# Moving the decay term of the RG-LRU recurrence (1 - loss) from ScalarE to VectorE

## What is computed

```
r = sigmoid(u @ w_rg + b_rg)
i = sigmoid(u @ w_ig + b_ig)
log_a = -LRU_C * r * softplus(-lru_lambda)
a = exp(log_a)
b = sqrt(-expm1(2 * log_a)) * (i * u)
h[t] = a[t] * h[t-1] + b[t]
lru_out = h * gelu(lru_y)
```

## Time and profile before

| | |
|---|---|
| median of 3 runs | 1619.98 us (1619.85 to 1621.9) |
| the profiled execution | 1621.06 us |
| its span, first to last instruction | 1619.2 us |
| TensorE busy | 1603.6 us, 99% |
| POOL busy | 1234.4 us, 76% |
| DVE busy | 905.0 us, 56% |
| ACT busy | 572.3 us, 35% |
| TensorE clock granted, mean | 0.997 of full |

### The profile page before, as it was taken

One profiled execution on the slowest core, in us unless ns is written; L12 is line 12 of the kernel. 1 busy time (PEld: TensorE's weight loads), 2 busy tenths in 40 slices (PEclk: granted clock), 3 DMA queues, 4 the chain that ended last, 5 costly groups with the idle time before them and its releaser, 6 DMA issues.

```text
span 1619.2 us, 24286 instructions
## 1 busy us (share of the span) xinstructions
PE 1603.6 (99%) x7390; PEld 1327.0 (82%) x7390; DVE 905.0 (56%) x1158; ACT 572.3 (35%) x1078; POOL 1234.4 (76%) x1330
## 2 busy tenths in 40 slices
PE   9999999999999999999999999999999999999997
PEld 7888888888888888888888878888888888788887
DVE  6565646652165666676622579677865558405502
ACT  4787335532226885255422244100010013102100
POOL 5787866777777788777777777788887778877875
PEclk9999999999999999999999999999999999999999
DMA  5445432233344454522333583344422222733632
GB/s 165 131 120 131 132 91 80 74 101 93 97 144 128 121 133 114 166 77 74 92 97 95 150 286 107 97 118 117 119 75 75 65 65 69 245 93 114 222 107 87
DMA packets 121462, 188.86 MB, mean 117 GB/s; under 512 B 13668, under 2 KB 45796, under 8 KB 121380
## 3 DMA queue, kind: packets, MB, share of 16 engines
q1 hardware_dynamic: 97476, 144.03, 32.1%
q10 hardware_dynamic: 23904, 43.79, 8.2%
HBM read 162.73 MB, written 17.56 MB: 111 GB/s over the span
## 4 chain that ended last, share of the span: by engine, by line
PE 90%; DVE 4%; issue 2%; ACT 2%; ACTq 0%; DMA 0%; POOL 0%; DVEq 0%; SPq 0%; POOLq 0%
PE ps L872 14%; PE ps L871 14%; PE ps L870 14%; PE ps L1128 8%; PE ps L1127 8%; PE ps L1129 8%; PE ps L1225 4%; PE ps L1226 4%; PE ps L1227 4%; PE ps L950 1%; PE ps L946 1%; PE ps L947 1%; PE ps L1038 1%; DVE rows L2152 1%; DVE rows_r L2311 1%
## 5 line engine op out<-in xcount | busy, mean ns | idle before, releaser
L688 POOL TENSOR_TENSOR w_lo<-w_raw,w_hi 128x512 fp32r<-128x512 f32 (+2 forms) x374 | 448.3, 1199 | 31.2
L685 POOL TENSOR_SCALAR w_hi<-w_raw 128x512 fp32r<-128x512 f32 (+2 forms) x374 | 242.5, 648 | 194.4 <-PE ps L872 127.3
L872 PE MATMUL ps<-h_hi,w_lo 128*128 128x512 f32 x672 | 263.8, 393 | 0.0
L871 PE MATMUL ps<-h_lo,w_hi 128*128 128x512 f32 x672 | 263.6, 392 | 0.0
L870 PE MATMUL ps<-h_hi,w_hi 128*128 128x512 f32 x672 | 262.1, 390 | 0.7 <-DVE g_h L1950 0.6
L870 PEld LDWEIGHTS ps<-h_hi,w_hi 128*128 128x128 f32 x672 | 126.2, 188 | 28.9 <-DVE g_h L1950 1.5
L871 PEld LDWEIGHTS ps<-h_lo,w_hi 128*128 128x128 f32 x672 | 126.2, 188 | 27.5
L872 PEld LDWEIGHTS ps<-h_hi,w_lo 128*128 128x128 f32 x672 | 126.3, 188 | 26.1
L1127 PE MATMUL ps<-t,w_hi 128*128 128x512 f32 x352 | 138.2, 392 | 0.6 <-POOL w_lo L763 0.5
L1128 PE MATMUL ps<-t,w_hi 128*128 128x512 f32 x352 | 138.7, 394 | 0.0
L1129 PE MATMUL ps<-t,w_lo 128*128 128x512 f32 x352 | 136.6, 388 | 0.0
(11 more groups left out here) (389 smaller groups left out, 4105.7 us busy)
## 6 DMA issues: line engine op xcount, KB each, us to landing
w_raw<-w_f SPq DMA_DIRECT2D x68, 256.0 KB, 3.2
w_raw<-w_step SPq DMA_DIRECT2D x64, 256.0 KB, 2.8
w_raw<-w_b SPq DMA_DIRECT2D x64, 256.0 KB, 3.1
w_raw<-w_d SPq DMA_DIRECT2D x64, 256.0 KB, 2.7
w_raw<-w_a SPq DMA_DIRECT2D x96, 128.0 KB, 2.1
w_raw<-w_q SPq DMA_DIRECT2D x32, 256.0 KB, 3.1
w_raw<-w_o SPq DMA_DIRECT2D x32, 256.0 KB, 3.1
mix_hl<-uc_hl ACTq DMA_DIRECT2D x24, 256.0 KB, 4.7
```

Source lines behind the costliest of these rows:

```text
L685: nc.gpsimd.tensor_scalar(w_hi[:, s, w], w_raw[:, s, w], 1.0, 0.0, ALU.mult, ALU.add).then_inc(w_hi_made, 1)
L688: nc.gpsimd.tensor_tensor(w_lo[:, s, w], w_raw[:, s, w], rd(w_hi[:, s, w]), ALU.subtract).then_inc(w_lo_made, 1)
L871: mm(out, w_hi[:, s, w], x_lo, start=False, stop=False)
L872: last = mm(out, w_lo[:, s, w], x_hi, start=False, stop=(k == total - 1))
```

## The change

The 20 `decay` activations leave ScalarE. DVE computes the same value, `g_r` x (-1) + 1 into `g_a`, with a tensor_scalar between amp and b, and counts `a_made` itself. It waits for `loss_made` and `amp_made` first, because it reads what loss writes and overwrites what amp reads. Nothing else moves, and no DMA is touched.

```
@@ ScalarE @@
-            def decay(h, j):
-
-                act.wait_ge(amp_made, j + KR * h + 1)
-                act.wait_ge(loss_made, j + KR * h + 1)
-                fn(g_a[:], g_r[:], ACT.Identity, bias=one_ap, scale=-1.0).then_inc(a_made, 1)
-
@@ ScalarE, recurrent @@
                     gate_root(h, j - 2)
                     mix(h, j)
-                    decay(h, j - 2)
                     gelu(h, j, n + 6, j % 4)
@@ ScalarE, kvq @@
                     gate_fns(h, 8 + p, n + 4 * p + 2)
                     gate_root(h, 8 + p)
-                    decay(h, 8 + p)
@@ DVE, recurrence @@
                 stt(g_r[:], g_a[:], 1.0, g_r[:], ALU.add, ALU.mult).then_inc(loss_made, 1)
                 stt(g_s[:], g_a[:], 1.0, g_s[:], ALU.add, ALU.mult).then_inc(amp_made, 1)
+                dve.wait_ge(loss_made, J + 1)
                 dve.wait_ge(amp_made, J + 1)
+                ts(g_a[:], g_r[:], -1.0, 1.0, ALU.mult, ALU.add).then_inc(a_made, 1)
                 dve.wait_ge(iu_made, J + 1)
                 stt(uc_of(q), g_s[:], 0.5, uc_of(q), ALU.mult, ALU.mult).then_inc(b_made, 1)
```

More of the change, by code:

```diff
@@ L1424, in gelu @@
                 fn(gy[:, q, :], ps[:, bank, :], ACT.Gelu_apprx_tanh).then_inc(gelu_made, 1)
[L1426 to L1430, removed]
             def lru_out_hi(h, j):
```

## The result

The changed kernel takes 1625.77 us, the median of 8 runs (1623.65 to 1627.36), against 1620.91 us for the kernel before on the same chip (8 runs, 1619.85 to 1621.9). The ratio is 1.003, with a 95% interval of 1.0019 to 1.0041: slower by 4.9 us. The forecast was 1624.2, in a range of 1620.9 to 1627.7, against a kernel before of 1619.98. The profiled execution of the changed kernel took 1624.75 us, with a span of 1622.9, 3.7 more than the 1619.2 of before.

The account below looks back on a forecast made before the run. TensorE was taken to bound the kernel, losing time only where it waits for tile 9's scan. 1.31 + 0.79 = 2.10 us a half, 4.2 us in all, gave a median of 1624.2 us, range 1620.9 to 1627.7.

Parts of the forecast that it names:

- What bounds the kernel: TensorE, 99% busy, waits at the second query tile for DVE's scan of tile 9, ending 0.06 us before the matmul.
- Rival 4: No effect: something else already holds TensorE at the second query tile, so the scan may come later; chance 0.05.
- The removal, and the step loop: Taking 20 decay off ScalarE, and 16 added DVE instructions in tiles 0 to 7: both costed at nothing.
- Rival 2: Faster: free ScalarE closes TensorE's weight-load gaps before the gates, at most 1.2 us back, 1618.8 us; chance 0.05.
- Tile 8: b 0.64 us late, the multiply after scan 8 loses its turn to POOL, 1.31 us late into ScalarE's chain.
- Rival 1: Not slower: DVE and POOL miss each other, +1.4 us, 1621.4; chance 0.18 including what lies up to the forecast.
- Tile 9: Loss, amp and the new instruction queue behind POOL: r + 0.34 us extra, 0.79 us with r 0.45.
- remainder r: Rest of a POOL turn that tile 9's queueing instructions meet first; between 0 and 1.10 us, taken as 0.45.
- Rival 3: Much slower: every queueing instruction meets POOL's TENSOR_TENSOR, +8.0 us, 1628.0; chance 0.10 including what lies above the forecast.
- Sum: Tile 8's 1.31 plus tile 9's 0.79: 2.10 us a half, 4.2 us for both.
- 2.4 and 2.8: Expected hold in us of the matmul at the second query tile, instead of 0.28 and 0.72.
- upper edge of +5.6: Top of the forecast's span of +3.3 to +5.6 us, for r from 0 to 1.10; the forecast's chance 0.62.

Follow-up runs that it names:

- e1: Kernel before, with 1 - loss moved to DVE for tiles 0 to 7 of each half only; 1621.11 us against 1620.83, ratio 1.0.
- e4: Kernel before, with 1 - loss moved to DVE for tile 9 only; one run, 1622.11 us.
- e2: Kernel before, with 1 - loss moved to DVE for tiles 8 and 9 only; 1626.12 us against 1620.83, ratio 1.0033.
- e9: One more profiled execution of the changed kernel, nothing edited; 1626.7 us.
- e8: Changed kernel, with the tensor_scalar of tiles 8 and 9 computed a second time into an unread gate tile; one run, 1627.55 us.
- e3: Kernel before, with 1 - loss moved to DVE for tile 8 only; one run, 1621.29 us.
- e10: One more profiled execution of the kernel before with 1 - loss on DVE in tiles 8 and 9 only, nothing edited; 1627.04 us.
- e7: Kernel before, decay still on ScalarE, with Exp of tiles 8 and 9 written to PSUM; 1618.81 us against 1620.53, ratio 0.9988.

## Why the prediction came out right

**What bounds the kernel.** Right. TensorE resumes 0.05 or 0.06 us after scan 9's end in before, in the changed kernel and in e1 to e4. Rival 4, something else holding TensorE there, is out.

**The removal, and the step loop.** Costed at nothing, and e1 measured nothing (interval 0.999 to 1.001). Rival 2 named the weight loads before the gates (L917), which stood still 1.2 us in before: in the changed kernel it is 0.8 us, but 1.7 in e1, the step loop alone, 1.4 in e2 and 0.2 in e9, the changed kernel again. That is no gain that the runs tell from chance, and e1's median is not lower than before's. ScalarE's `k_hi` in tile 8's time now starts at 162.19, straight behind the root, where before it stood behind `decay`, and no wait of TensorE is put down to it in either kernel. What "ScalarE: Activation LUTs" of the Trainium skill, Rules for kernel authors, says for this move (add and mul belong on VectorE) holds for the instruction alone, 0.43 us against 0.63, and not for this kernel, ratio 1.003.

**The instruction.** Predicted 0.42 us alone, measured 0.427 at its fastest. Predicted to queue, and it does: 0.66 and 1.33 us in the critical tiles, a second one 1.50 in e8.

**Tile 8.** Predicted: b and scan 0.64 us late, the multiply loses its turn, 1.31 us into ScalarE's chain. Measured: scan 8 4.17 - 3.53 = 0.64 late, the multiply 1.34 us long, `lru_hi` 6.04 - 4.75 = 1.29 late. That the multiply falls behind POOL's TENSOR_TENSOR, half of this term, was read from 0.07 us in the earlier trace rows; e3 shows it without tile 9's edit, behind a delay of 0.63 us, and no run tries a delay near 0.07. Rival 1 fell here.

**Tile 9.** Predicted 0.79 us, measured 4.34 - 3.61 = 0.73 from loss to the scan's start. The remainder r was 0.56 us, not 0.45, the two turns behind it were 0.40 and 0.91 instead of 1.55 in sum, and a started 0.11 us after amp's end, where I had it start 0.04 after, as b did before. These three misses, +0.11, -0.24 and +0.07, nearly cancel, and that is luck: with the measured r the rule that three queueing instructions pay r and two full turns gives 2.11 us, and they paid 1.87. Rival 3, a full long turn for each instruction, did not come: the turns alternate.

**Sum.** Predicted 2.10 us a half, measured 2.02 in each. I took 4.2 us for the pauses' growth and it is 3.97, because the second half's pause grew by 1.77 only. That half is as late as the first; but in before its value projection was shorter, 10.90 us against 11.31 (last section), which had made a pause of 0.72 out of the same lateness, and in the changed kernel both are 11.15. So the forecast "2.4 and 2.8" came as 2.48 and 2.49. (The forecast's upper edge of +5.6 is 5.5 by its own terms, 2 x (1.31 + 1.44); nothing hangs on it.)

**What was missed.** The clock. The prediction took a longer pause to cost its own length. That is not always so: the changed kernel took 1624.75 us with no fall and 1626.7 with two, e2 1625.84 with two, e10 1627.04 with one. The median of the changed kernel is 4.9 us above before's, the pauses give 4.0. That the remaining 0.9 us and the wider spread (3.7 us, against 2.0 for before) are such falls fits these profiles. It also fits the mean granted clock of the eight runs: the fastest, 1623.65 us, had 0.998, and three had 0.995 (1625.25, 1626.79 and 1627.36), where none of the 27 runs of before lies under 0.996. But that mean moves by 0.002 without a fall (0.996 in the changed kernel's profile, 0.998 in e8's, both with none), and a run's time shows no projection, so it is argued and not shown. The forecast lies 1.6 us below the measured 1625.77: 0.9 of it because before's own median stood at 1620.91 on this occasion and not at 1619.98, and 0.7 because the change cost 4.9 and not 4.2.

**What the runs add.** What costs is less the added instruction than where it stands. Its parts don't add: 0.74 and 0.65 alone, 2.02 together. And the same contention already cost the kernel before its two pauses, 1.0 us together, which e7 takes back.

## What to carry to other kernels

Where DVE and POOL both run dense, price a DVE instruction that has all its operands in SBUF by the turn of POOL that it may wait for, 0.2 to 1.1 us here for 0.43 to 0.69 us of work, and also price what stands behind it, since a delay can lose a later instruction its turn (0.63 us did so here; by the starts in the earlier trace rows anything above 0.07 would have). An operand in PSUM takes a two-source instruction out of this queue, even when POOL is left as it is (ratio 0.9988, interval 0.9979 to 0.9997, for two instructions in two tiles). An operation that runs off the critical path on an engine with idle time was free here; look for the serial chain before moving it to a faster one.

## What the runs showed of the hardware beside that

The granted clock can fall behind a pause of TensorE of 2.1 to 2.5 us, or not, in the same kernel and even in the same execution; a fall made a projection of 24 matmuls last 7.1 to 7.2 us instead of 5.61. What decides was not found.

The 256-column matmuls of the value projection come 0.118 us apart in some stretches and 0.113 in others. In before it is the first half that is slow and the second that is fast, and the projection lasts 11.31 and 10.90 us, with the granted clock at 1.00 in both; in e1 both are slow, in e4 the halves are the other way round. In both halves of the changed kernel the spacing went from 0.118 to 0.114 behind a pause of 0.08 to 0.09 us at the 38th of the 96 matmuls, next to the place where TensorE's program waits for scan 8. The rows below, of the kernel before, are the first matmul of the value projection and the first of the queries in each half: 175.08 - 163.77 = 11.31 us and 634.44 - 623.54 = 10.90. What decides was not found.

```profile
163.77 0.28 PE L988 MATMUL ps<-w_hi,h_hi 128*128 128x256 f32 x1
...
175.08 0.40 PE L870 MATMUL ps<-h_hi,w_hi 128*128 128x512 f32 x1
...
623.54 0.28 PE L988 MATMUL ps<-w_hi,h_hi 128*128 128x256 f32 x1
...
634.44 0.39 PE L870 MATMUL ps<-h_hi,w_hi 128*128 128x512 f32 x1
```
